# GDN decays from broadcast running sums, masked on GpSimd and exponentiated by rows and columns, with rounds and mixers laid out anew

## What is computed

```python
def reference(x, ...):
    for layer in range(2):
        h = _rmsnorm(x, norm_mix[layer])
        x = x + (_mlstm_retention_mixer if layer == 0 else _gated_deltanet_mixer)(h, ...)
        h = _rmsnorm(x, norm_ffn[layer])
        x = x + (silu(h @ w_gate) * (h @ w_up)) @ w_down
    return _rmsnorm(x, final_norm)

def _gated_deltanet_mixer(h, w_in, conv_w, a_log, dt_bias, norm_w, w_out):
    qkv, z, b_pre, a_pre = _split(h @ w_in, L1_SPLITS)
    qkv = silu(_causal_depthwise_conv(qkv, conv_w))
    q, k, v = ...                            # 16 q/k heads, 32 v heads of 128
    log_alpha = -exp(a_log) * softplus(a_pre + dt_bias)
    ...
    # _gated_delta_chunkwise:
    g_cum = cumsum(log_alpha)
    decay = exp(where(causal, g_cum[..., :, None] - g_cum[..., None, :], -inf))
    a = where(strict, (k * beta) @ k.T * decay, 0.0)
    sol = triangular_solve(a, [v * beta, k * beta * exp(g_cum)])
    attn = where(causal, q @ k.T * decay, 0.0)
    ...

def _mlstm_retention_mixer(h, positions, w_in, gate_bias, mlstm_norm, w_out):
    proj = h @ w_in                          # mLSTM and retention columns together
    # rotary by cos/sin of positions * inv_freq, head RMS norms, sigmoid and silu gates
    ...
    return concatenate([h_m, y_r]) @ w_out
```

## Time and profile before

| | us |
|---|---|
| median of 3 runs | 2826.89 |
| lowest, highest | 2826.2, 2827.94 |
| the profiled execution | 2829.2 |
| its span in the trace | 2827.4 |
| PE busy | 2784.0 (98%) |
| DVE busy | 1573.5 (56%) |
| ACT busy | 1373.8 (49%) |
| POOL busy | 75.4 (3%) |
| HBM traffic over the span | 177 GB/s |

### The profile page before, as it was taken

One profiled execution on the slowest core, in us unless ns is written; L12 is line 12 of the kernel. 1 busy time (PEld: TensorE's weight loads), 2 busy tenths in 40 slices (PEclk: granted clock), 3 DMA queues, 4 the chain that ended last, 5 costly groups with the idle time before them and its releaser, 6 DMA issues.

```text
span 2827.4 us, 37259 instructions
## 1 busy us (share of the span) xinstructions
PE 2784.0 (98%) x13652; PEld 2303.3 (81%) x13652; DVE 1573.5 (56%) x1946; ACT 1373.8 (49%) x1877; POOL 75.4 (3%) x54
## 2 busy tenths in 40 slices
PE   9999999999999999999999999999999999999998
PEld 7788788888888888877878787887888888888886
DVE  4554565545444444557686868665555454454444
ACT  5444555444444444456565767554454444444443
POOL 0000000000000000000010101000000000000000
PEclk9999999999999999999999999999999999999999
DMA  8464466666666666655353535555666666666664
GB/s 253 143 199 149 134 193 186 193 186 188 190 188 191 186 191 188 183 168 150 120 169 122 169 123 173 168 180 179 187 189 190 188 190 189 189 189 188 205 192 149
DMA packets 261554, 502.63 MB, mean 178 GB/s; under 512 B 20144, under 2 KB 20400, under 8 KB 261168
## 3 DMA queue, kind: packets, MB, share of 16 engines
q1 hardware_dynamic: 259792, 494.60, 58.2%
q10 hardware_dynamic: 816, 3.15, 0.3%
q0 software_dynamic: 816, 3.15, 0.3%
HBM read 495.59 MB, written 5.24 MB: 177 GB/s over the span
## 4 chain that ended last, share of the span: by engine, by line
PE 92%; DVE 5%; ACT 1%; issue 1%; DVEq 1%; DMA 0%; ACTq 0%; SPq 0%
PE acc L552 28%; PE acc L546 28%; PE acc L547 28%; PE aux L599 2%; PE aux L778 2%; DVE wlo L1441 2%; DVE arena L1863 1%; DVE arena L1860 1%; PE aux L784 1%; PE aux L772 1%; PE aux L758 0%; PE aux L751 0%; DVEq L1862 0%; ACT arena L1295 0%; DVEq L1829 0%
## 5 line engine op out<-in xcount | busy, mean ns | idle before, releaser
L1441 DVE TENSOR_TENSOR wlo<-wraw,whi 128x1024 fp32r<-128x1024 f32 x928 | 1152.1, 1250 | 1024.7 <-ACT whi L988 1017.0
L988 ACT ACTIVATE whi<-wraw 128x1024 fp32r<-128x1024 f32 x928 | 977.4, 1059 | 1151.2 <-PE acc L552 1073.8
L546 PE MATMUL acc<-whi,hT_hi 128*128 128x512 f32 x2624 | 1042.2, 397 | 0.9 <-ACT arena L998 0.5
L547 PE MATMUL acc<-whi,hT_lo 128*128 128x512 f32 x2624 | 1025.8, 391 | 0.0
L552 PE MATMUL acc<-wlo,hT_hi 128*128 128x512 f32 x2624 | 707.8, 392 | 14.7 <-DVE wlo L1441 14.3
L552 PEld LDWEIGHTS acc<-wlo,hT_hi 128*128 128x128 f32 x2624 | 493.6, 189 | 124.4 <-DVE wlo L1441 21.7
L546 PEld LDWEIGHTS acc<-whi,hT_hi 128*128 128x128 f32 x2624 | 494.8, 189 | 104.3 <-issue 1.7
L547 PEld LDWEIGHTS acc<-whi,hT_lo 128*128 128x128 f32 x2624 | 495.1, 189 | 101.7 <-issue 1.7
L546 PE MATMUL acc<-whi,arena 128*128 128x512 f32 x1088 | 427.4, 393 | 3.2 <-ACT whi L988 3.2
L547 PE MATMUL acc<-whi,arena 128*128 128x512 f32 x1088 | 425.1, 391 | 0.0
L552 PE MATMUL acc<-wlo,arena 128*128 128x512 f32 x1088 | 293.4, 392 | 0.0
(11 more groups left out here) (248 smaller groups left out, 1182.7 us busy)
## 6 DMA issues: line engine op xcount, KB each, us to landing
wraw<-in_l_w_in SPq DMA_DIRECT2D x304, 512.0 KB, 4.2
wraw<-in_l_w_gate SPq DMA_DIRECT2D x176, 512.0 KB, 3.7
wraw<-in_l_w_up SPq DMA_DIRECT2D x176, 512.0 KB, 3.6
wraw<-in_l_w_down SPq DMA_DIRECT2D x176, 512.0 KB, 4.2
wraw<-in_l_w_out SPq DMA_DIRECT2D x96, 512.0 KB, 4.6
o_rounds<-arena POOLq DMA_DIRECT2D x3, 1024.0 KB, 4.7
arena<-o_rounds ACTq DMA_DIRECT2D x3, 1024.0 KB, 6.1
x<-in_x SPq DMA_DIRECT2D x4, 512.0 KB, 7.0
```

The source lines that it names most:

```text
L546: nc.tensor.matmul(pair[m], hi[:, k, tok], wh, start=first, stop=False)
L547: nc.tensor.matmul(pair[m], lo[:, k, tok], wh, start=False, stop=False)
L988: nc.scalar.activation(whi[:, s, :], wraw[:, s, :], ACT.Copy).then_inc(hi_done, 1)
L1441: V.tensor_tensor(wlo[:, s, :], wraw[:, s, :], whi[:, s, :].bitcast(F32), ALU.subtract).then_inc(lo_done, 1)
```

## The change

**Decays.** A single matmul more, in the gates, gives the running sums transposed (64 rows, one for each head and chunk); ACT copies them out, and the sums themselves with both signs to `gate_t` (slots 1 and 9). POOL stores the 64x128 sums to DRAM once. For each round and chunk it loads the sums of eight heads to all 128 partitions (512 KB on chip) and subtracts or adds them to a mask of zeros and large negative numbers (128x1024). ACT takes the exponential of each head's 128x128 with a bias that differs by partition: minus row sums plus column sums is the exponent. EA and ET are made in that way independently. The matmuls L758, the multiplications L501, the transposes L765 and ACT's L1248 and L1252 are gone.

**Rounds.** The leaf is cut at `LEAF_CUTS` into eleven pieces, s = 10 to 20. The conv of Q and everything from the levels to V1 stands one slot later. The output squares are split over s = 36 and 38.

**Layer 0.** The sine and cosine are computed in the last body of the phase before. L0_SLOTS is set anew from slot 49 on, and ACT has its own table. The decay sums of the next mLSTM head are issued with `num_psum` of the one before, the head norm is done in two halves, the sigmoid stands one step earlier.

```diff
+            ("leaf_eye", LEAF * LEAF // 2), ("neg_t", 128)]
...
+    put("neg_t", neg.T)
...
 L0_SLOTS = ([0, 3, 5, 7, 9, 16, 17, 33, 35, 37, 39, 41, 43, 45, 47]
-            + [49, 50, 51, 53, 54, 55, 56, 57, 59, 60, 61, 62, 64, 65, 66, 67, 71, 73, 75, 76, 77])
+            + [49, 51, 53, 54, 56, 58, 59, 61, 63, 64, 66, 68, 69, 71, 73, 74, 75, 77])
+L0_ACT_SLOTS = [w if w == 0 or w > 69 else w + 1 for w in L0_SLOTS]
...
-DECAYS_AT = lambda r, c: (-2, 0)[c] if r == 0 else (-6, -5)[c]
+EA_AT = lambda r, c: (3, 4)[c] if r == 0 else (-3, -2)[c]
+ET_AT = lambda c: (12, 14)[c]
+FIRST_SLOT = -4
...
+LEAF_CUTS = (0, 3, 6, 9, 11, 14, 17, 19, 22, 25, 28, LEAF - 1)
...
+            def sums_of(r, c):
+
+                at = VH * c + HV * r
+                return sums_dram[at:at + HV, :].rearrange("(a h) n -> a (h n)", a=1).to_broadcast([P, HV * P])
+
             def decay_rows(r):
 
                 for c in range(M):
-                    nc.gpsimd.tensor_tensor(lam[:, c], C["after"].unsqueeze(1).to_broadcast([P, HV, P]),
-                                            of_round(1, r, c).unsqueeze(2).to_broadcast([P, HV, P]), ALU.mult
-                                            ).then_inc(lam_set, 1)
+                    pool.dma_start(EA[:, c].rearrange("p h n -> p (h n)"), sums_of(r, c)).then_inc(ea_loaded, 16)
+                for c in range(M):
+                    pool.wait_ge(ea_loaded, 16 * D_AT(r, M - 1))
+                    nc.gpsimd.tensor_tensor(EA[:, c], C["neg"][:, 0:P].unsqueeze(1).to_broadcast([P, HV, P]), EA[:, c], ALU.subtract
+                                            ).then_inc(ea_masked, 1)
+
+            def decay_columns(r):
+
+                if r:
+                    pool.wait_ge(end_psum, END_PSUM(r - 1, "o1"))
+                for c in range(M):
+                    pool.dma_start(ET[:, c].rearrange("p h n -> p (h n)"), sums_of(r, c)).then_inc(et_loaded, 16)
+                for c in range(M):
+                    pool.wait_ge(et_loaded, 16 * D_AT(r, M - 1))
+                    nc.gpsimd.tensor_tensor(ET[:, c], C["neg_t"].unsqueeze(1).to_broadcast([P, HV, P]), ET[:, c], ALU.add
+                                            ).then_inc(et_masked, 1)
...
                 if r < ROUNDS - 1:
                     pool.wait_ge(lev_psum, LEVEL_PSUM(r, "TT64_1"))
                     decay_rows(r + 1)
+                    decay_columns(r + 1)
                     pool.wait_ge(o_normed, r + 1)
...
                 nc.tensor.matmul(aux4[2][:, 0:64], C["upto"], la, start=True, stop=True)
+                nc.tensor.matmul(aux4[2][0:64, P:2 * P], la, C["upto"], start=True, stop=True)
...
-                def decays(c, to):
-                    pe.wait_ge(lam_set, D_AT(r, c))
-                    for n in range(2):
-                        mm = nc.tensor.matmul(to[:, n * NB:(n + 1) * NB], C["upto"], flat(lam[:, c, 4 * n:4 * n + 4, :]),
-                                              start=True, stop=True)
-                    mm.then_inc(d_psum, 1)
-
-                def decays_turned(c, to):
-                    pe.wait_ge(d_exp, D_AT(r, c))
-                    for h in range(HV):
-                        mm = nc.tensor.transpose(to[:, head(h)], EA[:, c, h, :], ident)
-                    mm.then_inc(eat_psum, 1)
...
-                if s == 23:
-                    pe.wait_ge(et_copy, D_AT(r, 1))
+                if s == 24:
+                    pe.wait_ge(gram_mask, GRAM_AT(r, "kk"))
...
+                def row_decays(c):
+                    act.wait_ge(ea_masked, D_AT(r, c))
+                    for h in range(HV):
+                        a = nc.scalar.activation(EA[:, c, h, :], EA[:, c, h, :], ACT.Exp, bias=of_round(1, r, c)[:, h:h + 1])
+                    a.then_inc(ea_exp, 1)
...
-                if 10 <= s <= 19:
-                    leaf(3 * (s - 10), 3 * (s - 10) + 3 if s < 19 else LEAF - 1)
-                if s == 19:
+                if 10 <= s <= 20:
+                    leaf(LEAF_CUTS[s - 10], LEAF_CUTS[s - 9])
+                if s == 20:
                     leaf_end()
...
+            def hook_a1(i, b, j):
+                hook_a(i, b, j)
+                if b == 1 and j == 1:
+                    next(mixer)
+            body("l0a", 1, 2, hook_a1)
...
-                head_norm(VM, OM, mnorm[:])
+                done(head_norm(VM, OM, mnorm[:], range(0, 2)))
+                head_norm(VM, OM, mnorm[:], range(2, 4)).then_inc(m_norm_late, 1)
```

199 lines of the change are left out of this document (106 added, 93 removed).

## The result

| | before | after |
|---|---|---|
| median, us (4 runs each, same chip) | 2826.55 | 2805.99 |
| lowest, highest | 2825.67, 2827.94 | 2804.33, 2807.48 |
| span of the profiled execution | 2827.4 | 2805.7 |

The ratio is 0.9926, with a 95% interval of 0.9914 to 0.9938. The kernel became 20.6 us faster. The forecast was 2797, 29.9 us faster, with a range of 2782 to 2810. The direction and the range were right; the gain is two thirds of the one expected, and a third of the sum has to be accounted for.

The account below looks back on a forecast made before the run. TensorE bounds the kernel, busy 2784.0 of 2827.4 us. Layer 0 8.1, L758 14.1, waits 1.8, first round's L765 1.8, leaf 6.2 + 1.6, clock 2.5, ET pair -6, new work -0.2 sum to 29.9: 2797 us, range 2782 to 2810.

Parts of the forecast that it names:

- L758, 14.1 us: Ahead of each DeltaNet round: eight removed groups of fp32 matmuls at 1.76 us each, all counted as gain, 14.1 us.
- L765 free in rounds 1 to 3: DeltaNet rounds 1 to 3: removed transposes gain 0 for 5.5 us, since the DVE works without pause to the leaf's end.
- The ET pair, 6 us: GpSimd's ET masks behind o1 stretch the DVE's wlo: 2.0 us, three times, 6 us given back, bounds 0 and 10.
- Clock, 2.5 us back: Half clock after leaf stops loses 6.6 us; only the first round's stop becomes short, so 2.5 us back, bounds 0 and 6.6.
- Layer 0, 8.1 us: Layer 0's sin/cos chain, mLSTM heads and mix stop holding TensorE: 8.1 us gained, bounds 4 and 10.
- The sin/cos term: Layer 0: the sin/cos chain, started some ten units earlier, no longer stops TensorE or halves its clock; 4.4 us gained.
- The heads and the mix: Layer 0: wider slots and halved head norm take away waits of 2.1 and 2.5 us; of 4.6, 0.9 stays.
- Leaf, 6.2 us: DeltaNet leaf in eleven units instead of ten: each leaf stop shrinks by 1.56 us, four times, 6.2 us.
- Layer 0 only moves its stops: Rival, chance 0.08: layer 0's gain of 8.1 us is given back, 2805 us.
- DVE chain takes all: Rival, chance 0.2: ET pair costs 3.4, longer stops halve the clock every round, half the leaf's gain is lost; 2808 us.
- Slower than before: Rival, chance 0.04: ACT's exponentials ahead of whi wait for loads and masks; loads landing after more than 30 us; 2836 at 31.

Follow-up runs that it names:

- e5: Changed kernel with the two groups of two fp32 matmuls of L758 issued again by TensorE ahead of rounds 1 to 3, results unread: 2817.25 us.
- e6: Changed kernel with eight transposes of a constant issued by TensorE in slots 7 and 8 of rounds 1 to 3, where L765 was: 2804.84 us.
- e4: Changed kernel with the leaf cut in ten pieces again, slots 10 to 19: 2809.33 us.
- e3: Changed kernel without GpSimd's two ET masks per round, loads kept, a sigmoid in place of the exponential: 2795.89 us.
- e9: e8 with the leaf cut in ten pieces again, slots 10 to 19: 2799.2 us.
- e8: Changed kernel with e1's edit and GpSimd's ET masks moved behind the leaf, exponentials in slots 28 and 30: 2790.37 us.
- e1: Changed kernel with ACT's layer 0 slots below 49 back where they stood in the kernel before: 2801.56 us.

## Why the prediction was partly right

Of the 29.9 us 20.6 came. The removed L758 and the sin/cos passage gave what was forecast, the ET masks stretched what they were said to stretch; their price, the clock and the leaf were sized wrongly, and the stop at the gates was not seen.

**L758, 14.1 us:** right. e5 gives 11.3 us for six of the eight groups, 10.6 by the sum.

**L765 free in rounds 1 to 3:** not shown. Put back, it left the median where it was (e6), but in e6's trace two thirds of its time stayed. The reason given was a DVE without a pause from o1 to the leaf's end, at which a TensorE that comes sooner waits longer. In the changed kernel the stop at L801 came first, and behind it wlo was 4 to 7 us ahead, so that TensorE was the bound again up to shortly before the leaf's end.

**The ET pair, 6 us:** the mechanism and the place of the masks were right (just behind o1, beside two wlo that took 2.7 us each on average instead of 1.2), the size was not. The prediction took 2.0 us out of 1.4 to 2.9 for the DVE's stretch and three rounds. The stretch was 5.41 - 2.35 = 3.1 us in each, the top of the range of a row that it had itself (2.9 to 3.4). It took no account of round 0, and none of the clock: the stop of 2.1 to 2.3 us that the stretch makes at L801 had a half clock behind it in each of rounds 1 to 3 of after (in the traces of e4, e5 and e6 in one round of the three). Taking the pair out gave 10.1 us (e3). And the place where TensorE would feel it was wrong. The prediction put what is late at the leaf's end, with stops of 3 us and more there in rounds 1 to 3. The taps of V0 were late first, since the transposes L801 wait for them in slot 5, while the stretched wlo themselves had 1.1 to 1.7 us in hand. At the leaf's end stops of 0.5 to 1.9 us were left.

**Clock, 2.5 us back:** wrong. The sum assumed that there would be one stop near 2 us fewer. In the stretches of five us the half clock lost 8.5 us of work in the trace of before (1.7 of it at the sin/cos passage) and 10.2 in the one of after. The stops went on being about as many, and a stop of 2.2 to 3.2 us had a half clock behind it in some executions and not in others: the wait at 1905 had one in after and none in before, the gates' stop of 2.2 us had one in after and none in the trace of e4, at the same length. In layer 1 this is 1.7 us lost instead of 2.5 gained, 4.2 us in all. That and the 4.1 us by which the ET pair was sized too small are not two separate parts of the missing 9.3: three of the five half clocks of layer 1 stand behind the stops at L801 and are in e3's 10.1 already. And the one at 1905 is there in one execution and not in another.

**Layer 0, 8.1 us:** 7.5 measured, but by two errors that cancel. The sin/cos term was 4.4 and gave 4.8; another 0.45 was there before it, from the program's start. The heads and the mix gave 6.3 instead of 3.7: the prediction counted the waits alone, 4.6 us, where the five stops took 0.3 us more each by the units' times, and it kept 0.9 back for a wait that did not come. Missing was the stop at the gates, 4.0 us, which the shift of ACT's whole table made. The prediction looked at the slots from 49 on, which the diff names, and not at what `w + 1` does to those below.

**Leaf, 6.2 us:** 3.3 by e4; by the passages of e9 about 4.1. Where the leaf's stop shrinks, the one behind conv Q, which waits for the same chain, grows by a part of it (in round 1 none in e9, 0.6 us in e8). The first round's stop, forecast at 2 us or less, is 2.29. TensorE's busy time, forecast near 2757, is 2764.0.

**The rivals.** "Layer 0 only moves its stops" (2805) came nearest in time, but by luck, since layer 0 gave 7.5 of its 8.1 us. "DVE chain takes all" (2808) came near as well, and in its mechanism too: the ET pair at its full size and half clocks that stay. It put them at the leaf. "Slower than before" was far away: the loads landed after a median of 5.5 us, between the 4.7 and the 8.2 of the earlier trace rows, and in the trace of after neither ACT nor TensorE waited for a mask. The prediction's estimate of 3.2 us for such a load, from the Trainium skill (DMA: Bandwidth & Descriptors, Anatomy of one DMA), is below what the row says, 5.5:

```profile
arena<-decay_sums POOLq DMA_DIRECT2D x16, 512.0 KB, 5.5
```

## What to carry to other kernels

When work moves from the engine that is the bound to one that idles, ask what that engine's instructions read, and lay them beside instructions of the others that they don't stretch: the ET masks cost 10 us beside wlo, next to nothing behind the wlo of conv Q (e8's 15.6 us are e1's 4.4 and e3's 10.1 and one more), and writes in their place cost nothing; the EA masks of the first round left the taps as they were. When a chain on a second engine is the bound over a stretch, list all who wait for it, in order of time; the first of them stops, the later ones then don't, and mending one stop shows the next. A table of slots that is shifted as a whole moves also the steps for which it was not meant; look at those where two engines hand small results back and forth.
